# One feed-forward layer of a two-block network: the second product in quarters, three of them by seven products of half blocks

## The reference

```python
h  = rmsnorm(x, norm_mlp_w) * (1.0 + sc2) + sh2          # 512 x 1024
ff = jnp.square(jax.nn.relu(h @ mlp_w1)) @ mlp_w2        # 1024 -> 4096 -> 1024
x  = x + g2 * ff                                         # g2: a row of the c_act @ ada_w product
```

## Time and profile before

| what | value |
|---|---|
| median of 3 runs | 1273.78 us (1273.72 to 1275.08) |
| span of the profiled execution | 1272.2 us |
| TensorE busy | 1239.2 us, 97% of the span |
| VectorE busy | 837.0 us, 66% |
| ScalarE busy | 580.9 us, 46% |
| GpSimd busy | 93.5 us, 7% |
| mean granted TensorE clock | 0.998 of full speed |

### The profile page before, as it was taken

How to read it: one execution, slowest core, us unless ns; L and a number is a source line. 1 busy time by engine, 2 the same in 40 slices (tenths; PEclk the granted TensorE clock), 3 DMA queues, 4 the chain that set the end, 5 groups by cost and what they waited for, 6 DMA issues and landing times.

```text
span 1272.2 us, 18645 instructions
## 1 busy us (share of the span) xinstructions
PE 1239.2 (97%) x6580; PEld 1014.3 (80%) x6580; DVE 837.0 (66%) x1270; ACT 580.9 (46%) x841; POOL 93.5 (7%) x144
## 2 busy tenths in 40 slices
PE   4999999999999999999999999999999999999998
PEld 3777778788888888888888888888888887777786
DVE  6889997857765333444444887665466668987822
ACT  3675445534444122433332655333233346978723
POOL 7022210000000000000000000110010000100000
PEclk9999999999999999999999999999999999999999
DMA  9688853426465333332333232334232232333321
GB/s 367 189 198 170 180 109 98 131 63 189 133 181 148 91 93 98 100 98 84 99 99 86 80 91 85 89 99 116 83 98 83 83 113 69 105 102 91 100 66 67
DMA packets 197981, 147.17 MB, mean 116 GB/s; under 512 B 6490, under 2 KB 178705, under 8 KB 197920
## 3 DMA queue, kind: packets, MB, share of 16 engines
q1 hardware_dynamic: 190448, 134.40, 35.4%
q0 software_dynamic: 6272, 10.91, 4.6%
q10 hardware_dynamic: 1200, 1.05, 0.3%
HBM read 135.59 MB, written 2.10 MB: 108 GB/s over the span
## 4 chain that ended last, share of the span: by engine, by line
PE 72%; DVE 16%; ACT 6%; issue 4%; DMA 1%; POOL 1%; DVEq 0%; ACTq 0%; SPq 0%; POOLq 0%
PE banks L421 22%; PE banks L423 22%; PE banks L422 22%; DVE w_lo L405 2%; ACT w_hi L393 2%; DVE score L1979 1%; DVE m L1976 1%; DVE xc L2513 1%; POOL e L2718 1%; DMA x_tok<-in_x 1%; DVE vh L2413 1%; DVE score L1962 1%; DMA hq<-in_ada_w 1%; PE banks L1119 1%; DVE sqb L1911 1%
## 5 line engine op out<-in xcount | busy, mean ns | idle before, releaser
L405 DVE TENSOR_TENSOR w_lo<-raw,w_hi 128x1024 fp32r<-128x1024 f32 x200 | 243.8, 1223 | 142.8 <-ACT w_hi L393 137.8
L421 PE MATMUL banks<-h_hi,w_hi 128*128 128x512 f32 x792 | 318.1, 402 | 2.3 <-DVE w_lo L405 0.8
L423 PE MATMUL banks<-h_hi,w_lo 128*128 128x512 f32 x792 | 309.0, 390 | 0.0
L422 PE MATMUL banks<-h_lo,w_hi 128*128 128x512 f32 x792 | 308.8, 390 | 0.0
L393 ACT ACTIVATE w_hi<-raw 128x1024 fp32r<-128x1024 f32 x200 | 209.6, 1052 | 195.4 <-PE banks L423 162.0
L421 PEld LDWEIGHTS banks<-h_hi,w_hi 128*128 128x128 f32 x792 | 148.8, 188 | 42.3 <-issue 8.3
L422 PEld LDWEIGHTS banks<-h_lo,w_hi 128*128 128x128 f32 x792 | 148.9, 188 | 33.4 <-issue 3.8
L423 PEld LDWEIGHTS banks<-h_hi,w_lo 128*128 128x128 f32 x792 | 148.8, 188 | 31.2
L421 PE MATMUL banks<-n_hi,w_hi 128*128 128x512 f32 x288 | 113.6, 395 | 0.9 <-DVE e L2475 0.9
L422 PE MATMUL banks<-n_lo,w_hi 128*128 128x512 f32 x288 | 112.3, 390 | 0.0
L423 PE MATMUL banks<-n_hi,w_lo 128*128 128x512 f32 x288 | 112.3, 390 | 0.0
(11 more groups left out here) (415 smaller groups left out, 1817.8 us busy)
## 6 DMA issues: line engine op xcount, KB each, us to landing
raw<-in_mlp_w SPq DMA_DIRECT2D x64, 512.0 KB, 3.9
raw<-in_a_w_in SPq DMA_DIRECT2D x48, 512.0 KB, 3.8
raw<-in_w_in SPq DMA_DIRECT2D x28, 512.0 KB, 4.4
raw<-in_ada_w SPq DMA_DIRECT2D x26, 512.0 KB, 4.6
raw<-in_b_w_in SPq DMA_DIRECT2D x24, 512.0 KB, 3.7
raw<-in_a_w_out SPq DMA_DIRECT2D x16, 512.0 KB, 3.7
raw<-in_b_w_out SPq DMA_DIRECT2D x12, 512.0 KB, 3.6
raw<-in_w_out SPq DMA_DIRECT2D x8, 512.0 KB, 4.3
```

What stands on the lines that cost most here:

```text
L405: dve.tensor_tensor(dst, src, hi, ALU.subtract).then_inc(split_lo, 1)
L421: pe.matmul(dst, l_hi, r_hi, start=first, stop=False, skip_group_check=onto)
L422: pe.matmul(dst, l_hi, r_lo, start=False, stop=False, skip_group_check=onto)
L423: return pe.matmul(dst, l_lo, r_hi, start=False, stop=last, skip_group_check=onto)
```

## The change

The hidden features are now worked in four quarters of 1024. The last quarter is computed as before: eight units up, then eight units down, 512 columns each. In the first three quarters the up part stays (eight units of 24 matmuls of 512 columns, one bank each), but the second product becomes, for each of the four pairs of output tiles (tile p and tile p + 4), a 2 x 2 block product done with seven products in place of eight. The left blocks are halves of the two weight tiles (A11, A12 from the upper tile, A21, A22 from the lower, 128 x 512 each), the right blocks are 4 row tiles x 256 tokens of the hidden activations (B11, B12, B21, B22). Seven products, each of 4 row tiles x 3 passes = 12 matmuls of 256 columns, use the left operands A11, A12, S4, A22, S1, S2, S3 and the right operands B11, B21, B22, T4, T1, T2, T3, where

- S1 = A21 + A22, S2 = S1 - A11, S4 = A12 - S2, S3 = A11 - A21, made by GpSimd (`weight_sums`, four instructions of 128 x 512 for each pair p),
- T1 = B12 - B11, T2 = B22 - T1, T3 = B22 - B12, T4 = B21 - T2, made by GpSimd (`hidden_sums`, four instructions of 128 x 256 for each of four pairs of hidden tiles).

Some products accumulate in the bank of an earlier one, so a bank is read in between: VectorE adds each product's running sum, scaled by the gate, into a half of an output tile of `xT` (`add_part`, 28 instructions of 128 x 256 for each quarter). Every operand form is split into high and low again: `seven_hi` on ScalarE and `seven_lo` on VectorE for 28 weight forms of 128 x 512, `forms_hi` and `forms_lo` for the seven hidden forms. A ring of eight slots of 512 columns holds the split weights; a unit takes two slots, a form one, and a step of the loops on ScalarE and VectorE makes what is to stand eight slots ahead. `TURN` is the order of the 28 products of a quarter.

Besides, several semaphores of the mixer are merged into fewer that count the same events in the same order (`conv_summed`, `conv_normed`, `conv_curved`, `o_curved`, and `hspread` in place of twelve), and the later tables of counts are shifted to suit.

The core of the diff:

```diff
+SEVENS = 3
+PRODUCT = {1: ("A11", B11), 2: ("A12", B21), 3: ("S4", B22), 4: ("A22", T4), 5: ("S1", T1), 6: ("S2", T2), 7: ("S3", T3)}
+TURN = ((1, 0), (2, 0), (1, 1), (2, 1), (5, 0), (6, 0), (5, 1), (3, 0), (6, 1), (7, 0), (3, 1), (4, 0),
+        (1, 2), (5, 2), (7, 1), (2, 2), (6, 2), (4, 1), (3, 2),
+        (1, 3), (5, 3), (7, 2), (2, 3), (6, 3), (4, 2), (7, 3), (3, 3), (4, 3))
...
+            def seven_free(m):          # SyncE: when a raw buffer may be loaded again
+                q, j = divmod(m, 16)
+                if j < 8:
+                    sp.wait_ge(f_lo, SLOT[q, j] + 2)
+                else:
+                    p, bottom = divmod(j - 8, 2)
+                    sp.wait_ge(f_lo, FORM_SLOT[q, p, "A22" if bottom else "A12"] + 1)
+                    sp.wait_ge(s_sum, sum_count(q, p, "S3"))
...
+            def part_waits(q, i, p):    # TensorE, ahead of a product
+                pe.wait_ge(f_lo, SLOT[q, i, p] + 1)
+                if i == 1:
+                    pe.wait_ge(evac, E_FF + 8 * q + 2 * p + 1)
...
+                else:
+                    pe.wait_ge(ff_x, X_READ[q, {6: 1, 3: 5, 7: 6, 4: 7}[i], p])
+                if (i, p) == (5, 0):
+                    pe.wait_ge(t_ready, 3 * (4 * q + 3) + 2)
+                if (i, p) == (7, 0):
+                    pe.wait_ge(t_ready, 3 * (4 * q + 3) + 3)
...
+            def seven_products(q):
+                for n, (i, p) in enumerate(TURN[0:4]):
+                    part_waits(q, i, p)
+                    for k in range(3):
...
+                        part(q, i, p, (k,))
+                pe.wait_ge(t_ready, 3 * (4 * q + 3) + 1)
+                for i, p in TURN[0:4]:
+                    part(q, i, p, (3,)).then_inc(f_used, 1)
+                for i, p in TURN[4:]:
+                    part_waits(q, i, p)
+                    part(q, i, p, range(4)).then_inc(f_used, 1)
...
+            for kind, q, n, made in steps():          # ScalarE
+                if kind == "product" and n == 0:
+                    forms_hi(4 * q + 3, 0)
+                for what in made:
+                    seven_hi(act, *what)
+                if kind == "product":
+                    if n == 0:
+                        forms_hi(4 * q + 3, 1)
+                    if n == 3:
+                        forms_hi(4 * q + 3, 2)
+                    continue
+                if n and n % 2 == 0:
+                    for f in range(3):
+                        forms_hi(4 * q + n // 2 - 1, f)
...
+                act.activation(relus[:, 2 * (pair % 2) + n % 2, :], banks[:, n, :], ACT.Relu).then_inc(evac, 1)
...
+            for kind, q, n, made in steps():          # VectorE
+                if kind == "product" and n == 0:
+                    forms_lo(4 * q + 3, 0)
+                for what in made:
+                    seven_lo(dve, *what)
+                if kind == "product":
+                    if n == 0:
+                        forms_lo(4 * q + 3, 1)
+                    if n == 3:
+                        forms_lo(4 * q + 3, 2)
...
+                    add_part(q, *TURN[n])
+                    continue
+                if n and n % 2 == 0:
+                    for f in range(3):
+                        forms_lo(4 * q + n // 2 - 1, f)
+                if q == 0:
+                    gate_tile(n)
...
+                dve.tensor_tensor(r, r, r, ALU.mult).then_inc(relu_sq, 1)
...
+            for q in range(SEVENS):                   # GpSimd
+                for k in range(3):
+                    hidden_sums(4 * q + k)
+                weight_sums(q, 0)
+                hidden_sums(4 * q + 3)
+                for p in range(1, 4):
+                    weight_sums(q, p)
```

More of the change, by code:

```diff
@@ new lines, in sum_at, with sum_count, makes @@
+        def sum_at(name):
+            return wsums[:, S_ORDER.index(name), :]
+        def sum_count(q, p, name):
+            return 4 * (4 * q + p) + S_ORDER.index(name) + 1
+        def makes(last, slots):
+            for q in range(SEVENS):
+                for j in range(8):
+                    if last < SLOT[q, j] + 2 <= slots:
+                        yield "unit", q, j, SLOT[q, j]
+                for i, p in TURN:
+                    if last < SLOT[q, i, p] + 1 <= slots:
+                        yield "form", q, (p, PRODUCT[i][0]), SLOT[q, i, p]
+            for j in range(LEAD):
+                if last < SLOTS_END + 2 * j + 2 <= slots:
+                    yield "plain", 0, j, SLOTS_END + 2 * j
@@ new lines, in steps, with first_free @@
+        def steps():
+            last = 2 * LEAD
+            for q in range(SEVENS):
+                for j in range(8):
+                    yield "unit", q, j, list(makes(last, SLOT[q, j] + SLOTS))
+                    last = max(last, SLOT[q, j] + SLOTS)
+                for n, (i, p) in enumerate(TURN):
+                    yield "product", q, n, list(makes(last, SLOT[q, i, p] + SLOTS))
+                    last = max(last, SLOT[q, i, p] + SLOTS)
+        def first_free(eng, n, size):
+            if n < SLOTS:
+                eng.wait_ge(w_used, U_FF - RING + n // 2 + 1)
+            else:
+                eng.wait_ge(f_used, n - SLOTS + size)
@@ L1026, in _ @@
             last.then_inc(ws_summed, 1)
[L1029 to L1037, removed]
             def second_gate_columns():
@@ L1041, in second_gate_columns @@
                 pe.wait_ge(wsum_made, 2)
[L1042 to L1054, removed]
-                down = (U_FF + 32 * half + 16, 2, KT, hid_hi, hid_lo, X_FF + KT * half, H_HID + 16 * half)
-                if half == 0:
-                    residual_product(0, *down, between={0: second_gate_columns})
-                with pe.Fori(1 - half, 4) as i:
-                    residual_product(i, *down)
+                pe.wait_ge(evac, E_FF + 7)
@@ new lines, in second_gate_columns, with ff_three, bank_read @@
+                columns(lambda j: acc2[:, j * P:(j + 1) * P], 6)
+            def ff_three(n, k, bank, first, last):
+                r = slice((k % 4) * P, (k % 4 + 1) * P)
+                return three(pe, banks[:, bank, :], slot(w_hi, n + k // 4)[:, r], slot(w_lo, n + k // 4)[:, r],
+                             h_hi[:, k, :], h_lo[:, k, :], first, last)
+            def bank_read(q, j):
+                if q:
+                    pe.wait_ge(ff_x, X_READ[q - 1, *BANK_LAST[j]])
+                elif j in (4, 5):
+                    pe.wait_ge(wsum_made, j - 3)
@@ new lines, in seven_unit, with part @@
+            def seven_unit(q, j):
+                n = SLOT[q, j]
+                pe.wait_ge(f_lo, n + 2)
+                bank_read(q, j)
+                for k in range(KT):
+                    last = ff_three(n, k, j, k == 0, k == KT - 1)
+                last.then_inc(f_used, 2 + 4 * ((q, j + 1) == SKIP))
+            def part(q, i, p, ks):
+                n, moving = SLOT[q, i, p], PRODUCT[i][1]
+                dst = part_bank(i, p)
+                opens = i in (1, 2, 5)
+                for k in ks:
+                    r = slice(k * P, (k + 1) * P)
+                    w1_, w0_ = slot(w_hi, n)[:, r], slot(w_lo, n)[:, r]
+                    m1_, m0_ = form_hi[:, k, moving, :], form_lo[:, k, moving, :]
+                    last = three(pe, dst, w1_, w0_, m1_, m0_, opens and k == 0, k == 3, True)
+                return last
@@ new lines, in _ @@
+            for j in range(KT):
+                pe.wait_ge(split_lo, U_FF + j + 1)
+                pe.wait_ge(ff_x, X_READ[SEVENS - 1, *BANK_LAST[j]])
+                for k in range(KT):
+                    last = three(pe, banks[:, j, :], unit(w_hi, U_FF + j, P)[:, k, :], unit(w_lo, U_FF + j, P)[:, k, :],
+                                 h_hi[:, k, :], h_lo[:, k, :], k == 0, k == KT - 1)
+                last.then_inc(w_used, 1)
+            pe.wait_ge(evac, E_FF + 28)
+            residual(U_FF + KT, KT, 1, KT, hid_hi, hid_lo, X_FF, H_HID)
```

382 lines of the change are left out of this document (287 added, 95 removed).

## The result

The changed kernel takes 1322.81 us (median, 1322.01 to 1325.51) against 1274.36 us: a ratio of 1.0381, 95% interval 1.0366 to 1.0396. It is 48 us slower. 1317 was forecast, with 1286 to 1333 as the range.

A forecast was written before the change was run, and what follows sets the result against it. TensorE's columns were taken to bound the feed-forward part: 1273.8 us, less 9.8 for fewer columns, plus 53.4 of waits from chains with GpSimd and VectorE blocking each other, gives 1317, range 1286 to 1333.

The forecast's parts named there:

- The gain: Second product in three quarters: 336 matmuls of 256 columns take 40.25 us in place of 43.5, saving 9.8 us in all.
- The chains: Two new chains making operands and additions keep TensorE waiting in three quarters: 25.7 us without blocking, 53.4 with it.
- the walk: All five queues followed in order with traced durations and 0.05 us hand-overs: 53.4 us of TensorE waits with blocking.
- the clock: Granted clock falling after gaps in the feed-forward part: 1 to 2 us per large fall, left out of the sum.
- chain B: Third pair's lower weight tile waits for a buffer; VectorE's addition queues behind its split: 2.4 us before product eleven without blocking.
- chain A: From last hidden tile's square through GpSimd's sums to low parts of T1 and T2: product five waits 3.0 us without blocking.
- The block: GpSimd's sums and VectorE's instructions with two SBUF operands never overlap, until 0.2 us before GpSimd's end: waits 53.4 for 25.7 us.
- rival 1: No blocking between GpSimd's sums and VectorE: 25.7 us of waits, 1290 us, 1285 to 1300; chance 0.22.
- Rival 2: The chains are hidden behind TensorE's work in the feed-forward part: 1264 to 1271 us; chance 0.10.
- The first quarter: Gate tiles on VectorE get in the way: 23.9 us of waits, 8.6 of them before the gate columns.

The follow-up runs named there:

- e10: e8's kernel with the additions of the first two pairs' second products moved behind that of the first pair's seventh product: 1270.04 us, ratio 0.9952.
- e3: Changed kernel with useless filler matmuls on TensorE ahead of its long waits: 1323.42 us, ratio 1.0373 to the kernel before.
- e4: Changed kernel with the third and fourth pair's weight tiles loaded into four buffers of their own: 1310.06 us.
- e9: Changed kernel with VectorE's additions ahead of splits, which come three products later, and the low parts of T3 and T4 two products later: 1313.49 us.
- e5: Changed kernel with the T sums on VectorE, right behind the square, in place of GpSimd: 1309.68 us.
- e1: Changed kernel with each GpSimd sum replaced by two clears of about the same length that read nothing: 1295.11 us.
- e2: Changed kernel with each GpSimd sum replaced by one short clear that reads nothing: 1278.19 us, ratio 1.0022 to the kernel before.
- e6: Changed kernel with the eight gate sums on VectorE cut to one column each: 1315.58 us.
- e8: Changed kernel with e4, e5 and e9 together, squares on ScalarE, gate tiles first in their step, S sums on VectorE too: 1273.1 us, ratio 0.9971.

## Why the prediction was right, and where it was off

**The gain** was priced rightly: 0.12 us per matmul of 256 columns, and 40.9 us for a phase once the waits are gone (e10).

**The chains** came where the walk had them. In the second quarter its low parts of T1 and T2 at 11.12 and its addition at 24.77, each with a hand-over of 0.05, put product five at 11.17 us into the phase and eleven at 24.82; the trace has 11.30 and 25.16. In e3's third phase, where the clock was 1.00, the six steps between useful matmuls that hold a wait are 1.9, 3.6, 2.2, 2.7, 3.1 and 1.4 us longer than 0.12, for the 1.9, 3.5, 2.2, 2.8, 3.1 and 1.2 walked. e4 and e9 show the two halves of chain B, the late buffer and the addition queued behind a split; e5 shows chain A, together with the T sums' block.

**The block** was the choice that mattered, 1317 against 1290. e1 gives 1295 without it, where rival 1 had 1290, and the two directions read from the earlier trace rows are in the trace as lengthened sums and splits. Its length, 0.2 us less than GpSimd's recorded time, is 0.14 less in this trace. The time alone does not choose between 0.2 and the full length: 1322.8 lies midway between 1317 and 1328.

**The size** was 5.4 us short of the 1317.4 before rounding. 4.3 us of it are inside the part: 398.0 us against 350.1 - 9.8 + 53.4 = 393.7. 2.4 are in the product phases (52.3, 56.1 and 55.8 for 51.9, 55.0 and 55.0) and 1.9 between the last unit and the first product, where the wait was as walked (12.4 for 3.7 + 8.6), but the 16 gate columns took 3.4 us at a clock of 0.50 for 1.7 before. The mis-sized term is thus above all the clock, which the sum left out: 1.7 us at the gate columns, and 1.7 in the phases, which take 162.4 us with the filler of e3 for 164.2, where the walk has 161.8. The other 0.9 us stay open; that each block lasts 0.06 us longer than walked is one candidate, and no run separates it. The prediction gave no reason for leaving the clock out. Its price of 1 to 2 us for each fall charged slow matmuls that end in a wait, and my expectation for e3, 1317, made the same mistake: half pace made steps without a wait 13.5 us longer, and the listed waits are 39.9 us in place of 53.4 largely for that reason, but e3 shows that little of it is lost, because the chains set the next start. The rest lies outside the part: the median is 2.5 us over the profiled span here, and 1.6 were assumed.

**Rival 2** (chains hidden, 1264 to 1271) is not what this order does. e2 shows how far GpSimd alone was from it: with sums of half a microsecond and no block the time is 1278, since VectorE's order still makes waits. e10 shows that it can be had with other orders and buffers and with all sums on VectorE. **The first quarter** was seen rightly as the worst place; e6 puts 7 us of the 12.4 on the gate tiles; without the block (e1) 3.7 are left, so the two overlap. What makes the rest was not separated.

## What to carry to other kernels

Fewer columns on TensorE pay only if every chain that makes the new operands is shorter than the work that covers it: walk each chain through all queues, in order, before the busy shares are believed. Work for an idle GpSimd is not free where VectorE has instructions with two SBUF operands: here a sum of 512 columns cost 1.29 us there and held VectorE up as well, while VectorE makes it in 0.60 (start to start, e8). In a queue put first what frees a bank or a buffer that somebody waits for, and last what is wanted many products later.

## What the runs showed of the hardware

- GpSimd and VectorE held each other up in both directions where both read SBUF (GpSimd's sums 1584 ns for 1289, VectorE's splits 999 for 690). Clears by GpSimd of the same length (1.28 us) left the splits at 684 ns. The one that was held up went on 0.13 to 0.17 us before the recorded end of the other.
- In stretches with gaps of 2 to 12 us the granted clock was 0.59 to 0.94, and matmuls of 256 columns came 0.21 us apart in place of 0.12; with filler in the gaps it was 0.96 to 1.00 over the product phases. Half pace behind a wait cost next to nothing where another wait followed (13.5 us of it, and 2.1 us of the part's time).
